# One order of the recurrence's normalisation moved behind the next head's gates, and three smaller edits

## The reference, cut to what matters

```
u = rms_norm(h, g_norm) @ w_in;  q, f, i, z = split(u)
q = silu(q);  fg = lb + (1 - lb) * sigmoid(f);  k = 1 - fg;  v = i
b = cumsum(log(fg)) within chunks of 64
A = causal(einsum(q*exp(b-b_mid), k*exp(b_mid-b)))
o = A @ v + (q*exp(b)) @ S_prev          # S_prev: states from chunk to chunk
o = rms_norm(o per head, g_out);  h += (o * silu(z)) @ w_out
...
qh = rms_norm(x, norm2_g) @ peer_w_q;  sub = qh . sub_keys;  top 16, twice
```

## Time and profile before

| | |
|---|---|
| time, median of 3 runs | 3206.47 us (3203.27 to 3208.0) |
| time of the profiled execution | 3206.9 us |
| its span, first to last instruction | 3205.1 us |
| TensorE | busy 3106.4 us, 97% of the span |
| VectorE, ScalarE, GpSimd | 58%, 51%, 21% |
| mean granted clock of TensorE | 0.981 of full |
| DMA | 157 GB/s over the span |

### The profile page before, as it was taken

How to read it: one execution, slowest core, us unless ns; L and a number is a source line. 1 busy time by engine, 2 the same in 40 slices (tenths; PEclk the granted TensorE clock), 3 DMA queues, 4 the chain that set the end, 5 groups by cost and what they waited for, 6 DMA issues and landing times.

```text
span 3205.1 us, 63948 instructions
## 1 busy us (share of the span) xinstructions
PE 3106.4 (97%) x25426; PEld 3023.9 (94%) x25426; DVE 1866.1 (58%) x3255; ACT 1624.9 (51%) x2600; POOL 675.3 (21%) x292
## 2 busy tenths in 40 slices
PE   8999998999999999889999999999999999999999
PEld 8999998999999898768999999999999999999999
DVE  5545555645444357756677788644447865554444
ACT  5666765466677642365444443444444444444443
POOL 3333332444434342203444310000000000000000
PEclk9999998999999899999999999999999999999999
DMA  5433433444433354324455544455554455555554
GB/s 194 139 137 131 144 131 111 167 171 169 146 132 133 113 183 149 111 79 145 162 181 183 173 147 142 170 184 184 183 184 165 152 174 184 183 182 183 183 183 157
DMA packets 72287, 506.59 MB, mean 158 GB/s; under 512 B 7904, under 2 KB 10592, under 8 KB 11232
## 3 DMA queue, kind: packets, MB, share of 16 engines
q1 hardware_dynamic: 71584, 503.09, 45.3%
q10 hardware_dynamic: 576, 1.72, 0.2%
HBM read 502.69 MB, written 2.10 MB: 157 GB/s over the span
## 4 chain that ended last, share of the span: by engine, by line
PE 90%; DVE 5%; ACT 3%; issue 2%; DMA 0%; DVEq 0%; SPq 0%; ACTq 0%
PE bank L448 13%; PE bank L450 12%; PE bank L449 12%; PE bank L2150 4%; PE bank L2151 4%; PE bank L2152 4%; PE banks L2151 4%; PE banks L2150 4%; PE banks L2152 4%; PE bank L462 3%; PE banks L1945 3%; PE banks L1946 3%; PE bank L1946 3%; PE bank L1945 3%; PE banks L1947 3%; PE bank L1947 3%
## 5 line engine op out<-in xcount | busy, mean ns | idle before, releaser
L425 ACT ACTIVATE whi<-raw 128x1024 fp32r<-128x1024 f32 x898 | 940.9, 1057 | 1059.4 <-PE bank L450 446.8
L432 DVE TENSOR_TENSOR wlo<-raw,whi 128x1024 fp32r<-128x1024 f32 x667 | 811.5, 1228 | 477.9 <-ACT whi L425 476.9
L432 POOL TENSOR_TENSOR wlo<-raw,whi 128x1024 fp32r<-128x1024 f32 x231 | 614.7, 2661 | 1079.6 <-ACT whi L425 1074.0
L448 PE MATMUL bank<-xa_hi,whi 128*128 128x272 f32 (+1 forms) x2048 | 604.8, 295 | 2.9 <-DVE wlo L432 1.8
L450 PE MATMUL bank<-xa_hi,wlo 128*128 128x272 f32 (+1 forms) x2048 | 596.9, 291 | 0.0
L449 PE MATMUL bank<-xa_lo,whi 128*128 128x272 f32 (+1 forms) x2048 | 595.2, 291 | 0.0
L448 PEld LDWEIGHTS bank<-xa_hi,whi 128*128 128x128 f32 x2048 | 394.9, 193 | 7.6 <-issue 2.7
L449 PEld LDWEIGHTS bank<-xa_lo,whi 128*128 128x128 f32 x2048 | 396.3, 193 | 0.7
L450 PEld LDWEIGHTS bank<-xa_hi,wlo 128*128 128x128 f32 x2048 | 393.8, 192 | 0.0
L448 PE MATMUL bank<-xb_hi,whi 128*128 128x256 f32 (+1 forms) x1152 | 332.4, 289 | 6.5 <-DVE f_qg L999 6.1
L450 PE MATMUL bank<-xb_hi,wlo 128*128 128x256 f32 (+1 forms) x1152 | 327.9, 285 | 0.0
(11 more groups left out here) (417 smaller groups left out, 6684.6 us busy)
## 6 DMA issues: line engine op xcount, KB each, us to landing
raw<-in_w SPq DMA_DIRECT2D x251, 1024.0 KB, 4.8
raw<-in_v SPq DMA_DIRECT2D x128, 1024.0 KB, 5.3
raw<-in_u SPq DMA_DIRECT2D x96, 1024.0 KB, 4.8
hT<-in_hT SPq DMA_DIRECT2D x4, 544.0 KB, 8.6
out<-hT SPq DMA_DIRECT2D x8, 256.0 KB, 3.2
r_keys<-in_keys ACTq DMA_DIRECT2D x1, 1024.0 KB, 5.0
c_mask<-in_masks ACTq DMA_DIRECT2D x1, 320.0 KB, 2.9
params<-in_params SPq DMA_DIRECT2D x1, 238.5 KB, 2.6
```

The costliest lines, as they stand in the source:

```text
L425: act.activation(whi[:, (2 * t.q + half) % 4, :], raw[:, t.q, half * 1024:(half + 1) * 1024], ACT.Copy).then_inc(w_hi_done, 1)
L432: eng.tensor_tensor(wlo[:, t.q, at], raw[:, t.q, at], whi[:, slot, :].bitcast(F32), ALU.subtract).then_inc(w_lo_done[half], 1)
L448: te.matmul(ps, hi, x[0][:, kk, cols], start=(kk == 0), stop=False)
```

## The change

PE, ACT and DVE get a new order in the body of the recurrence. On PE the sum of squares of h - 2 moves from behind t0 to behind the attention products. The product with zeros goes; the first product into `B_O` starts the accumulation instead. On ACT the Square of h - 2 goes behind the sigmoids and logarithm of p; the logarithm and exponential for `rn` go behind the split for t3 and the keys' copies; the copy into `xb_hi` goes behind the split for the next t0. On DVE `on` and `mm` go behind the evacuation of t1, the split and the masked attention; the evacuation of t2 and the split of the next t0 follow at once; `xb_lo` and `zs` come after these.

`route_tensor` no longer waits for `rinv_done`; DVE does, ahead of its routing. The tensor of zeros becomes an unused gap of the same size, and `token` has 24 columns in place of 32, so that every tensor behind it (`whi`, `hT`, `xb`, `xa` and all of the stages' own) lies 32 bytes lower. `table_for` takes its scratch column among ACT's own.

```diff
-        zt = tensor(ctx, "zeros", [P, P], F32R)
-        token = tensor(ctx, "token", [P, 32])
+        tensor(ctx, "gap", [P, P])
+        token = tensor(ctx, "token", [P, 24])
...
 (tensor)
-                if within(h - 2, HEADS):
-                    te.wait_ge(osq_done, h - 1)
-                    te.matmul(SUM[:, 0:L], con("ones"), g.osq[:], start=True, stop=True).then_inc(osum_done, 1)
                 if within(p, HEADS):
                     te.wait_ge(evacuated, 4 * p + 3)
...
                     last.then_inc(att_done, 1)
+                if within(h - 2, HEADS):
+                    te.wait_ge(osq_done, h - 1)
+                    te.matmul(SUM[:, 0:L], con("ones"), g.osq[:], start=True, stop=True).then_inc(osum_done, 1)
...
-                    te.matmul(B_O[:, 0:L], zeros_l, xa[0][:, 0, :], start=True, stop=False)
...
-                            last = te.matmul(B_O[:, cs], g.v[rows, n, :], g.att[rows, att_cols(c_)], start=False,
+                            last = te.matmul(B_O[:, cs], g.v[rows, n, :], g.att[rows, att_cols(c_)], start=(c_ == 0),
...
 (scalar)
-                if within(h - 2, HEADS):
-                    act.wait_ge(o_done, h - 1)
-                    act.activation(g.osq[:], B_O[:, 0:L], ACT.Square).then_inc(osq_done, 1)
                 if within(p, HEADS):
                     act.wait_ge(evacuated, 4 * p + 4)
...
                     act.activation(g.logf[:], g.fg[:], ACT.Ln).then_inc(logf_done, 1)
+                if within(h - 2, HEADS):
+                    act.wait_ge(o_done, h - 1)
+                    act.activation(g.osq[:], B_O[:, 0:L], ACT.Square).then_inc(osq_done, 1)
...
-                if within(h - 2, HEADS):
-                    act.wait_ge(osum_done, h - 1)
-                    ch.link(act.activation(g.lnv[:], SUM[:, 0:L], ACT.Ln, bias=con("eps"), scale=1.0 / P))
-                    act.activation(g.rn[:], g.lnv[:], ACT.Exp, scale=-0.5).then_inc(orn_done, 1)
                 if within(h, HEADS):
                     split_hi(act, t[2].next())
                 (the copies into kst)
                 if within(h - 2, HEADS):
+                    act.wait_ge(osum_done, h - 1)
+                    ch.link(act.activation(g.lnv[:], SUM[:, 0:L], ACT.Ln, bias=con("eps"), scale=1.0 / P))
+                    act.activation(g.rn[:], g.lnv[:], ACT.Exp, scale=-0.5).then_inc(orn_done, 1)
+                if within(h, HEADS):
+                    split_hi(act, t[3].next())
+                if within(h - 2, HEADS):
                     act.wait_ge(m_done, h - 1)
                     lone(act)
                     act.activation(at3(xb[0], h - 2), one3(g.mm[:]), ACT.Copy).then_inc(mhi_done, 1)
-                if within(h, HEADS):
-                    split_hi(act, t[3].next())
...
 (vector: on and mm of h - 2 move from behind factors_done to behind masked_done, then)
+                if within(h, HEADS):
+                    evac(t[2], g.vr)
+                    split_lo(ve, t[3].next(), 0)
+                if within(h - 2, HEADS):
                     ve.wait_ge(mhi_done, 16 + h - 1)
                     (xb_lo, then zs)
-                if within(h, HEADS):
-                    evac(t[2], g.vr)
-                    split_lo(ve, t[3].next(), 0)
...
         def route_tensor(te, ch):
-            te.wait_ge(rinv_done, 3)
             te.wait_ge(evacuated, T_PEERQ)
...
 (route_vector)
+            ve.wait_ge(rinv_done, 3)
             ve.tensor_copy(e.iota[:], con("iota"))
```

More of the change, by code:

```diff
@@ L377, in lone @@
                 eng.tensor_tensor(token[:, k:k + 1], con("one"), con("one"), ALU.add)
-        tables_asked = [0]
         def table_for(act, function):
-            tables_asked[0] = (tables_asked[0] + 1) % 8
-            k = 24 + tables_asked[0]
+            token_at[act] = (token_at[act] + 1) % 8
+            k = 8 * list(token_at).index(act) + token_at[act]
             act.activation(token[:, k:k + 1], con("one"), function)
@@ L592, in out_pool @@
             ch.run(body, 0, 3, 1)
-        zeros_l = zt[:]
         masks_f, masks_c, masks_r = sem("masks_f"), sem("masks_c"), sem("masks_r")
@@ L789, in hgrn_vector @@
         def hgrn_vector(ve, ch):
-            ve.memset(zt[:].bitcast(F32), 0.0).then_inc(preset, 1)
-            ve.memset(g.att[:], 0.0)
+            ve.memset(g.att[:], 0.0).then_inc(preset, 1)
             ve.wait_ge(inputs_in, IN_ALL)
@@ L856, in body @@
                     ve.tensor_tensor(g.qe[:], g.qs[:], g.e_cum[:], ALU.mult).then_inc(factors_done, 1)
[L857 to L861, removed]
                 if within(h, HEADS):
@@ L871, in body @@
                 if within(h - 2, HEADS):
+                    ve.wait_ge(orn_done, h - 1)
+                    ch.link(ve.scalar_tensor_tensor(g.on[:], B_O[:, 0:L], par("a_out_norm", h - 2), g.rn[:],
+                                                    ALU.mult, ALU.mult))
+                    ve.tensor_tensor(g.mm[:], g.on[:], g.zs[:], ALU.mult).then_inc(m_done, 1)
+                if within(h, HEADS):
+                    evac(t[2], g.vr)
+                    split_lo(ve, t[3].next(), 0)
+                if within(h - 2, HEADS):
                     ve.wait_ge(mhi_done, 16 + h - 1)
```

## The result

The changed kernel takes 3179.2 us (median of 4 runs, 3176.21 to 3179.3), the one before 3205.55 beside it: a ratio of 0.992, 95% interval 0.9909 to 0.9932, or 26 us less.

What follows compares the result with a forecast made beforehand. TensorE, busy 97% of the span, was taken as the bound. Zeros -1.95, tail +0.5, routing -3.2 and heads' clock -4.6 sum to -9.25 us from the median 3206.47: say 3197.5 us, eight in ten between 3189 and 3207.

Steps and rivals of the forecast that it cites:

- Tensors 32 bytes nearer: All matmuls: the new addresses were taken as 0, though 1 ns on each would be 25 us either way.
- rival 5: The 32 bytes change matmuls or loads: 3180 or 3225 us, chance 0.12, more of it without sizeable effect.
- if a projection's matmuls have another spacing than now: Projections: one of three signs that would show the prediction wrong; the spacing was 0.13 us.
- Zeros: Recurrence: dropping the product with zeros saves 0.13 us per head, 1.95 us over 15 heads.
- The order in the loop: Recurrence heads: moving the sum of squares and the root neither gains nor loses, taken as 0.
- the root's cover: Recurrence heads: the moved root's result is ready 1.3 us before TensorE wants it at line 701.
- rival 4: The root comes too late and TensorE waits at line 701 in 14 heads: for instance 3214 us, chance 0.07.
- The tail: Body 16: gates start earlier but sum of squares and root end later, cost +0.5 us, bounds -1 to +1.5.
- Routing: Start of routing: TensorE's 2.46 us wait for the reciprocal goes, and most of the slow clock behind it; -3.2 us.
- no clock of 0.58 behind it: Start of routing: a sign that would show the prediction right, no slowed clock behind line 504.
- the upper bound: Start of routing: both the wait and the clock's drop go, 2.5 + 1.1 = 3.6 us.
- The clock in the heads: Recurrence: 0.13 us shorter heads break the two slow, one not pattern; five slow of 15 for eight, -4.6 us.

Runs made afterwards that it cites:

- a_shift_64: The changed kernel with whi and all behind it 32 bytes lower still, 64 below the kernel before; 3177.67 us, ratio 0.9915.
- a_no_shift: The changed kernel with token back at 32 columns, so every edit but the 32-byte shift; 3198.35 us, ratio 0.998.
- b_no_zeros: The kernel before without the product with zeros, nothing else; 3198.35 us, ratio 0.9981.
- best_64: The changed kernel with whi and all behind it 64 bytes lower than before, and body 16's sum of squares and root in their old places; 3175.18 us, ratio 0.9904.
- b_route_only: The kernel before with only the wait for the reciprocal moved from TensorE to VectorE at the start of routing; 3198.89 us, ratio 0.9978.
- a_all_64: The changed kernel with token as before and everything from rinv on 32 bytes higher, restoring the distances of the kernel before; 3197.95 us, ratio 0.9977.
- b_order_only: The kernel before with only the recurrence's new order on three engines; zeros, routing wait and addresses kept; 3209.79 us, ratio 1.0009.
- b_shift_only: The kernel before with token at 24 columns, so whi and all behind it lie 32 bytes lower, no instruction moved; 3182.74 us, ratio 0.9929.
- b_coefhi_32: The kernel before with coef_hi alone 32 bytes higher; 3198.87 us, ratio 0.9975.
- b_rest_only: The kernel before with all behind whi 32 bytes higher and whi where it was; 3191.2 us, ratio 0.9957.
- b_rest_64: The kernel before with a gap of 64 bytes between whi and hT, moving hT, xb, xa and low coefficients; 3208.55 us, ratio 1.0019.
- b_whi_64: The kernel before with whi alone 64 bytes lower; 3173.92 us, ratio 0.9915.

## Why the prediction was wrong

**The step that failed** is the term of the sum "Tensors 32 bytes nearer ... I take 0". The prediction had bounded it by 1 ns a matmul, 25 us, and had it as rival 5 at 3180 us with a chance of 0.12. It measured 22 us by itself, 0.9 ns over 25426 matmuls. The average hides where it lies: in the steady part of the experts' stages it is 1.1 to 1.3 ns (from 119.5 to 118.3 in the up stage, from 119.1 to 117.8 in the down stages), in the recurrence next to nothing. The argument for 0 was that the input blocks of one projection lie 1088 bytes apart at an even spacing of 0.13 us. From one block to the next the weights move by 512 bytes and the input by 1088, so the row compares distances in steps of 576 bytes and none that is off by 32; it is from the recurrence, where these 32 bytes do least; and it is written to 0.01 us, ten times the 1 ns in question. It was an argument from a row that couldn't show the effect, and didn't carry a chance as low as 0.12: of the ten other placements in the table, seven gain at least 10 us by their medians (one of them, `a_shift_64`, with the other edits in it). The prediction's own sign, "if a projection's matmuls have another spacing than now", is the one that came.

**The rest of the sum**, -9.25 us, stands by itself in `a_no_shift`: 6.5 us less, between 3.2 and 9.6 by its interval. By its terms:

- Zeros: 0.12 to 0.13 us a head as worked out, 1.9 us. That `b_no_zeros` gains 6.5 I put down to the clock, with three slow heads in its trace in place of eight. That is argued from one execution, the fastest of ten, and not shown.
- The order in the loop, taken as 0: no wait of TensorE appeared, the root's cover was 1.2 us for 1.3, and rival 4 didn't come. The sum of squares costs 0.66 us in the chain for 0.46 at the old place, yet a head grows by only 0.02 us. By its median the order alone costs 2.3 us, its interval from none to 6.
- The tail, +0.5: from the last head's products by state to the next 19.64 us before and 20.06 after, +0.42. The mechanism is the one described; that the gates gained and the root lost more can be had back is what `best_64` shows.
- Routing, -3.2: the wait went, and with only this edit 3.9 us went with it. In the changed kernel the drop of the clock stayed, 0.52 over 3.5 us, though TensorE doesn't stand behind line 502; "no clock of 0.58 behind it" failed as a sign. The prediction counted one idle stretch here and there are two: the 2.01 us ahead of the sum of squares stay in all six kernels without the wait, of which three (the changed one, `a_shift_64`, `best_64`) show the drop and three (`b_route_only`, `a_no_shift`, `a_all_64`) don't. What decides between them no run shows. The Trainium skill, TensorE: Matmul & The Clock Gate, § What's actually happening, has activity release the throttle. The trace of `b_route_only` agrees with it; that of the changed kernel shows that to drop this one wait is not enough for the upper bound.
- The clock in the heads, -4.6 for five slow heads: the changed kernel's trace has four, -6.1. But one trace's count is no property of a kernel: `b_route_only` is the kernel before up to routing and has 6 where that has 8, `a_no_shift` has 7, `b_order_only` 10 with heads of the same two lengths to 0.03 us, and from run to run a kernel's time moves by some 10 us (3202.8 to 3212.5 for the kernel before on one chip). The working by a pattern that closes or doesn't gave a number for what one trace samples, and no run here bears it out.

**The order of the terms.** The prediction called the heads' clock its largest and least certain term. The addresses were both.

**What stays open.** That the distances of the tensors TensorE reads to their neighbours set the spacing of its matmuls is shown: by `b_shift_only`, by `a_all_64`, where only the distances are restored, and by `b_coefhi_32`, where only the stage that reads the moved tensor changes its pace. Which distances are slow is not: neither multiples of 64 nor of 128 fit all rows of the table, and the two down stages of `b_rest_only` and of `b_rest_64` differ with one set of addresses, once with the first at 117.8 ns and the second at 120.0, once the other way round. Why a distance matters no profile shows. In these stages ScalarE and VectorE read `raw` (the next tile of weights) and write `whi` and `wlo` meanwhile. The traces give no sign that this is it: sorted by what ran at the time, the spacing in the steady part of the first down stage is 119.1 ns in the kernel before with ScalarE alone, VectorE alone, both or neither at work, and 115.5 to 115.6 in `b_whi_64`. A run without these accesses was not made, and the loads by DMA run all the while.

## What to carry to other kernels

A tensor made smaller ahead of others is an edit of its own, even by 32 bytes: measure it apart from the rest before the gain is put down to an order of instructions. Where TensorE issues back to back and sets the time, a few placements of its weight tensors against its moving ones are worth a run each; whi alone 64 bytes lower gave 30 us here, where the whole change gave 26. The length of a stage mixes its pace with slow matmuls at its start and with what follows its last matmul: compare paces within the steady part. A slowed clock that comes and goes between runs is a spread to be averaged over, and its count in one trace is no term of a sum.

## What the runs showed of the hardware

The spacing of back-to-back matmuls of 256 columns at full clock ran from 115.6 ns (`b_whi_64`) to 120.0 (`b_rest_64`) in the steady part of a down stage, with no instruction changed. The page's mean durations, whose ends are modelled, follow it unevenly among matmuls that do equal work: high coefficients by `whi` 280 and 283 ns in the two kernels, low ones by `whi` 278 and 285, high ones by `wlo` 277 and 283:

```profile
L2153 PE MATMUL bank<-e_coef_hi,wlo 128*128 128x256 f32 x1024 | 283.5, 277 | 0.0
```
```profile
L2153 PE MATMUL bank<-e_coef_hi,wlo 128*128 128x256 f32 x1024 | 290.2, 283 | 0.0
```

Within one execution TensorE is busy 5.3 us longer in the second down stage of `b_rest_only` than in the first, and 6.8 us shorter in that of `b_rest_64`; in the kernel before it is 1.4 us shorter, which is the slow matmuls at the start of the first, and the pace is 119.1 ns in both. So something besides the addresses takes part, and it was not found.
